# An encoder trunk in two blocks: the second block cut into three 368-column chunks that hold the sample tokens behind a zero gap

## The reference, cut to what matters

```python
def layer(x, pool_buf, conv_buf, ffn_buf, offset, ...):      # x: (B, T, 1024)
    h = rmsnorm(x, g_pre_mix)
    z = h @ w_in                                             # 2048 columns: v | gb | gc | u
    pooled, new_pool = multiscale_pool(z_v, pool_buf, offset) # trailing means of 2, 4, 8, 16 tokens
    ya = einsum(pooled, pool_mix) * pool_scale
    conv_out, new_conv = causal_dwconv(gc * u, conv_buf, conv_w)   # 3 taps
    yb = gb * conv_out
    mix = concat([head_rmsnorm(ya, 4, ...), head_rmsnorm(yb, 8, ...)]) @ w_out
    x = x + rmsnorm(mix, g_post_mix)
    h = rmsnorm(x, g_pre_ffn)
    up, new_ffn = causal_dwconv(h @ w_up, ffn_buf, ffn_conv_w)     # 3 taps over 5632 columns
    f = (silu(up[..., :2816]) * up[..., 2816:]) @ w_down
    x = x + rmsnorm(f, g_post_ffn)
    return x, new_pool, new_conv, new_ffn
```

## Time and profile before

| | |
|---|---|
| median of three runs | 3019.7 us |
| the profiled execution | 3020.9 us |
| its span on the slowest core (core 7) | 3019.3 us |
| PE busy | 2792.1 us (92%), 13920 matmuls |
| DVE busy | 1917.6 us (64%) |
| ACT busy | 1505.4 us (50%) |
| POOL busy | 1004.0 us (33%) |
| share of PE in the chain that ended last | 80% |

### The profile page before, as it was taken

How to read it: one execution, slowest core, us unless ns; L and a number is a source line. 1 busy time by engine, 2 the same in 40 slices (tenths; PEclk the granted TensorE clock), 3 DMA queues, 4 the chain that set the end, 5 groups by cost and what they waited for, 6 DMA issues and landing times.

```text
span 3019.3 us, 45417 instructions; the slowest of 8 cores (2990.8 to 3019.3 us)
## 1 busy us (share of the span) xinstructions
PE 2792.1 (92%) x13920; PEld 1259.8 (42%) x13920; DVE 1917.6 (64%) x2636; ACT 1505.4 (50%) x3141; POOL 1004.0 (33%) x1092
## 2 busy tenths in 40 slices
PE   3999999999999999996899998899988899988998
PEld 1444444444444444443344443344433444433443
DVE  3787368745776478745677545777357774467763
ACT  3754366435644375445644346544356443464443
POOL 3344054414343144404333224433043331343320
PEclk9999999999999999998988999988999999998889
DMA  8684267525673359456473334733154632437321
GB/s 165 102 143 77 46 108 127 92 49 102 101 121 67 67 95 156 77 122 122 71 115 60 50 65 77 123 66 61 33 102 82 104 64 44 84 66 126 59 41 61
DMA packets 203853, 263.75 MB, mean 87 GB/s; under 512 B 147040, under 2 KB 148832, under 8 KB 203616
## 3 DMA queue, kind: packets, MB, share of 16 engines
q0 software_dynamic: 52992, 189.82, 38.4%
q1 hardware_dynamic: 150624, 71.03, 11.3%
HBM read 406.70 MB, written 9.29 MB: 138 GB/s over the span
## 4 chain that ended last, share of the span: by engine, by line
PE 80%; DVE 6%; issue 5%; ACT 4%; DMA 2%; POOL 1%; SPq 0%; DVEq 0%; ACTq 0%; POOLq 0%
PE psum_all L366 80%; DVE sb_r L400 3%; ACT sb_r L384 3%; DMA sb_h<-sb_hs 2%; DVE sb_r L389 1%; ACT sb_tp L384 1%; POOL sb_r L389 1%; DVE sb_hs L400 0%; POOL sb_x L389 0%; DVE sb_tp L400 0%; ACT sb_ss L384 0%; SPq L516 0%; DMA sb_g<-gains 0%; DVEq L150 0%; DVE sb_x L389 0%
## 5 line engine op out<-in xcount | busy, mean ns | idle before, releaser
L366 PE MATMUL psum_all<-sb_h,sb_w 128*128 128x512 bf16 (+1 forms) x9600 | 1872.0, 358 | 141.4 <-DMA sb_h<-sb_hs 64.3
L366 PEld LDWEIGHTS psum_all<-sb_h,sb_w 128*128 128x128 bf16 x9600 | 838.5, 101 | 1147.6 <-issue 485.6
L400 DVE SCALAR_TENSOR_TENSOR sb_r<-psum_all,sb_vec,sb_r 128x1023 f32<-128x1023 f32 (+2 forms) x1216 | 1027.4, 851 | 327.4 <-ACT sb_cf L404 246.0
L389 POOL TENSOR_TENSOR sb_r<-sb_r 128x1088 bf16<-128x1088 f32 (+16 forms) x416 | 637.9, 1533 | 1223.1 <-ACT sb_r L384 808.1
L366 PE MATMUL psum_all<-sb_w,sb_r 128*128 128x512 bf16 (+1 forms) x4080 | 893.1, 381 | 13.3 <-ACT sb_r L384 11.1
L384 ACT ACTIVATE sb_r<-psum_all,sb_vec 128x1024 f32<-128x1024 f32 (+4 forms) x768 | 539.7, 738 | 346.8 <-PE psum_all L366 345.9
L366 PEld LDWEIGHTS psum_all<-sb_w,sb_r 128*128 128x128 bf16 (+1 forms) x4080 | 400.9, 99 | 496.6 <-issue 29.2
L384 ACT ACTIVATE sb_r<-sb_r 128x1024 f32<-128x1024 f32 (+6 forms) x376 | 314.3, 839 | 430.4 <-DVE sb_r L389 398.2
L414 POOL DMA_DIRECT2D sb_w<-wts x360 | 206.9, 575 | 497.9 <-PE psum_all L366 457.2
L400 DVE SCALAR_TENSOR_TENSOR sb_tp<-psum_all,sb_ss,sb_g 128x1024 f32<-128x1024 f32 x136 | 174.3, 1282 | 307.7 <-ACT sb_ss L384 271.5
L400 DVE SCALAR_TENSOR_TENSOR sb_r<-sb_r,sb_vec 128x512 bf16<-128x512 f32 (+3 forms) x320 | 250.1, 802 | 105.6 <-ACT sb_r L384 97.3
(11 more groups left out here) (44 smaller groups left out, 543.4 us busy)
## 6 DMA issues: line engine op xcount, KB each, us to landing
sb_w<-wts POOLq DMA_DIRECT2D x360, 512.0 KB, 6.6
sb_g<-gains SPq DMA_DIRECT2D x33, 512.0 KB, 5.3
sb_x<-xp SPq DMA_DIRECT2D x16, 512.0 KB, 5.4
yp<-sb_x SPq DMA_DIRECT2D x16, 512.0 KB, 2.7
sb_h<-sb_hs SPq DMA_TRANSPOSE x136, 3.1
sb_pm<-pm POOLq DMA_DIRECT2D x8, 128.0 KB, 3.0
sb_tp<-gains SPq DMA_DIRECT2D x1, 512.0 KB, 9.2
sb_vec<-vecs SPq DMA_DIRECT2D x1, 312.0 KB, 22.9
```

Of the source, the lines that this page charges most:

```text
L366: P.op(PE, lambda h: h.matmul(oa, la, ra, start=start, stop=stop), reads=[lv.r(llo, lhi), rv.r(rlo, rhi)], writes=[ov.r(olo, ohi)])
L389: P.op(eng, lambda h: h.tensor_tensor(oa, aa, ba, op), reads=[av.r(alo, ahi), bv.r(blo, bhi)], writes=[ov.r(olo, ohi)])
L400: P.op(DVE, lambda h: h.scalar_tensor_tensor(oa, aa, sc, ba, op0, op1), reads=reads, writes=[ov.r(olo, ohi)])
```

## The change

In the second block the sample now stands in the same column range as the prompt, behind a gap of 16 columns of zeros: 1024 + 16 + 64 = 1104 columns, cut into three chunks of 368. The separate sample parts and `u_sample` are gone. Mixer history of the sample is copied into the gap, so pooling and short convolution run over it as over any other column. For the up projection a chunk's product has 370 columns: two columns before the chunk are recomputed, so the taps read all they need from PSUM and the edge terms between chunks go (`lead_edges` is used in the first block alone). Two last columns of `sb_h` from the first block are kept in `sb_hh` for that purpose. The first two chunks of a pair of PSUM banks are read by one instruction, as 2 x 368 columns; the third chunk lies in bank 6 or 7 alone. The second block has four lead pairs, whose first part is two chunks and whose second part is the third chunk.

Also changed: the order of channel groups (1, 3, 2, 0 in place of 3, 2, 1, 0); the order of tiles in the second block (the sample's is seventh of nine, it was fifth); the last token tile's pre norm of each layer is deferred into the first step of the next z stage, and at the start of the program and between the blocks four tiles are deferred into its first steps; banks are taken by least recent use, and the first block's up projection and both down projections use all eight; the first weight loads wait for transposes, not for token loads.

```diff
-NLEAD = 5
+NLEAD = (5, 4)
+JORDER = (1, 3, 2, 0)
+GAP = 16
+KN = 368
...
+        gap3 = h3[:, :, HO + 1024:HO + 1024 + GAP]
+        P.op(DVE, lambda h: h.memset(gap3, 0.0), writes=[hv[kt].r(HO + 1024, HO + 1024 + GAP) for kt in range(KT)])
...
-                ts.insert(4, dict(x=8, a=1024, p=64, src=xs_d[:, :], dst=ys_d[:, :]))
+                ts.insert(6, dict(x=8, c=1024 + GAP, p=DSEQ, src=xs_d[:, :], dst=ys_d[:, :]))
...
+            bounds = (0, 512, 1024) if bi == 0 else (0, KN, 2 * KN, 3 * KN)
...
+                sched = ((0, 0), (1, 0), (0, 1), (1, 1), (0, 2), (2, 0), (1, 2), (2, 1), (3, 0), (2, 2), (3, 1), (3, 2))
...
+                    m.a_gc()
+                    if si < len(deferred):
+                        for f in deferred[si]:
+                            f()
...
-                def u_sample(i, ws, fg, fvv):
-                    for t_, fv in ((0, fg), (1, fvv)):
-                        jt = i + NPAIR * t_
-                        bk = banks[6 + t_]
-                        u_mm(i, ws, t_, bk, 0, 1024, 64)
-                        conv_ew(fv, 1024, 64, bk, 0, jt, (b_e, 88 + 2 * jt), (b_stf, (l * 44 + jt) * 2))
...
+                def conv_b(fv, k0, cnt, b0, jt):
+
+                    ps = V(b_ps, b0 * PBANK, cnt * PBANK, F32)
+                    out = spread(fv, k0 * KN, KN, cnt, KN)
+                    ract(out, shifted(ps, 2, cnt), AF.Copy, scale=vcol(l, W2 + jt))
...
+                    for w, sh in ((W1, 1), (W0, 0)):
+                        rstt(out, shifted(ps, sh, cnt), vcol(l, w + jt), out, ALU.mult, ALU.add)
+                    if k0 + cnt == 3:
+                        a = 1024 + GAP
+                        tt(DVE, (fv, a, a + 2), (fv, a, a + 2), (V(b_e, 2 * jt, 2, F32), 0, 2), ALU.add)
...
+                        if part != 1:
+                            pk = take_pair(range(3))
+                            for k in range(2):
+                                u_mm(ws, t_, banks[2 * pk + k], HO - 2 + k * KN, KN + 2)
+                            conv_b(fv, 0, 2, 2 * pk, jt)
+                        if part != 0:
+                            bk = take_bank((6, 7))
+                            u_mm(ws, t_, banks[bk], HO - 2 + 2 * KN, KN + 2)
+                            conv_b(fv, 2, 1, bk, jt)
...
-                    if not last_layer:
+                    if last_layer:
+                        final_tile(t, "pre", t["dst"])
+                    elif last:
+                        deferred = [[lambda t=t: pre_tile(t, "pre")]]
+                    else:
                         pre_tile(t, "pre")
```

More of the change, by code:

```diff
@@ L209, in unit_table @@
     tab = []
[L210 removed]
+    for j in JORDER:
         tab += [("z", 2 * j), ("z", 2 * j + 1)]
@@ L400, in stt, with __init__, spread, ract @@
             P.op(DVE, lambda h: h.scalar_tensor_tensor(oa, aa, sc, ba, op0, op1), reads=reads, writes=[ov.r(olo, ohi)])
+        class Raw:
+            def __init__(self, ap, rs):
+                self.ap, self.rs = ap, list(rs)
+        def spread(v, lo, n, cnt, stride):
+            o_ = v.off + lo
+            ap = v.b.t[0:v.p, o_:o_ + cnt * stride].rearrange("p (b c) -> p b c", c=stride)[:, :, 0:n] \
+                if o_ + cnt * stride <= v.b.width else None
+            assert ap is not None and v.dt == F32
+            return Raw(ap, [(v.b, o_ + k * stride, o_ + k * stride + n) for k in range(cnt)])
+        def ract(out, in_, func, scale=None, bias=None):
+            kw, reads = {}, list(in_.rs)
+            if scale is not None:
+                kw["scale"] = scale
+                if isinstance(scale, tuple):
+                    kw["scale"] = scale[0]; reads.append(scale[1])
+            if bias is not None:
+                kw["bias"] = bias[0]; reads.append(bias[1])
+            P.op(ACT, lambda h: h.activation(out=out.ap, in_=in_.ap, func=func, **kw), reads=reads, writes=out.rs)
+        def rstt(out, in0, scalar, in1, op0, op1):
+            P.op(DVE, lambda h: h.scalar_tensor_tensor(out.ap, in0.ap, scalar[0], in1.ap, op0, op1),
+                 reads=in0.rs + in1.rs + [scalar[1]], writes=out.rs)
         def copy(eng, out_ap, out_r, in_ap, in_r):
@@ new lines, in __init__ @@
+                        self.yp = yp[i % 2]
+                        self.sc = sqc[i % 2]
+                        self.sp = sqp[i % 2]
+                    def a_v(self):
+                        c, vb = self.c, self.vb
+                        va = 16 + c["c"]
+                        act((vb, va, va + self.n), (self.bv, 0, self.n), AF.Copy)
+                        with_s = c["last"] and bi == 1
+                        if with_s:
+                            state_in(POOL, b_stp, 15, self.j, vb, 16 + 1024 + GAP)
@@ L743, in d_fin, with do @@
                             ALU.mult, ALU.mult)
[L745 to L750 removed]
+                p1 = p2 = None
+                def do(p, *names):
+                    if p is not None:
                         for nm in names:
                             getattr(p, nm)()
[L754 to L755 removed]
+                for si, (pos, ci) in enumerate(sched):
+                    j = JORDER[pos]
+                    if ci == 0:
@@ new lines, in next_fa, with conv_a @@
+                def next_fa():
+                    fa_ctr[0] += 1
+                    return fa[fa_ctr[0] % 4]
+                def conv_a(fv, lo, n, src, jt, edge=None, tail=None):
+                    act((fv, lo, lo + n), (src, 0, n), AF.Copy, scale=vcol(l, W2 + jt))
+                    if tail is not None:
+                        copy(ACT, tail.ap(0, 2), tail.r(0, 2), src.ap(n - 2, n), src.r(n - 2, n))
+                    for w, sh in ((W1, 1), (W0, 2)):
+                        stt((fv, lo + sh, lo + n), (src, 0, n - sh), vcol(l, w + jt), (fv, lo + sh, lo + n),
+                            ALU.mult, ALU.add)
+                    if edge is not None:
+                        tt(DVE, (fv, lo, lo + 2), (fv, lo, lo + 2), (edge, 0, 2), ALU.add)
```

500 lines of the change are left out of this document (232 added, 268 removed).

## The result

The changed kernel takes 2908.6 us in the profiled execution and 2910.9 in a second one; its ratio to the kernel before is 0.9652, with a 95% interval of 0.9614 to 0.9691. In the other two of its four executions the cores of one die ran at a mean clock of 0.84 to 0.87, so the ratio leaves these two out, and all that follows is read from cores and stretches at full clock. Faster was forecast with 0.83, the time as 2880 us within 2845 to 2965.

The account below looks back on a forecast made before the run. The prediction took a loop through ACT and DVE to bound the second block's u. Its terms, -120 + 9 - 25 - 7 - 2 = -145, gave 2876 us on core 7; it forecast 2880 us for the slowest core, within 2845 to 2965.

Parts of the forecast that it names:

- The bound and the loop: Second block's u: PE waits for a loop through ACT and DVE, some 29 us a stage; the change leaves PE the bound.
- u, -120: Second block's four u stages: 684 us against 804.0, since the loop goes and PE is the bound.
- the third chunks: Lead pairs in second block's u: PE waits because only banks 6 and 7 serve; 0 to 5.6 us, 2.5 taken.
- DVE's backlog: Second block's u: 2 us a stage for DVE being behind from the norms.
- o and the start of u, +9: Second block, from o to u: 6.2 us wait for a tile's norm and transpose, 1.5 us low clock; bounds -18 to +25.
- z of layers 1 to 3, -25: Second block's z: 75 us each, 225 against 250.3, with a first pool-map wait of 4.3 us; bounds -50 to 0.
- z between the blocks, -7: Stage between the blocks: 90 us against 97.0, with waits of 16.4 us in place of 17.4; bounds -20 to +5.
- The rest, -2: Program start, first-block z and down projections: earlier chunk 0 offset by deferred tiles, last pre norm gives little; bounds -12 to +10.
- d, 0: Down projection stages: no change, since they are PE's, 343.4 of 345.6 us.
- The clock falls: Two rivals: low clock again in u, +34 us a stage, chance 0.22; or in all the second block, 3190 us, 0.04.
- DVE and ACT become the bound: Rival in u: each piece of a two-piece read costs its own 0.21 us; 2930 us if z keeps its time; chance 0.10.
- The loop stays: Rival in u: SiLU still waits, now on g's third chunk; u at 190 us, kernel 2956; chance 0.04.

Follow-up runs that it names:

- the first experiment: Kernel before, with only the sample piece of g moved ahead of v's work in the second block's u: 2926 to 2929 us, ratio 0.97.
- the eight banks: Changed kernel, with the second block's lead third chunks allowed any of eight PSUM banks instead of 6 and 7: 2881.5 and 2882.6 us, ratio 0.955.
- the products put ahead: Changed kernel, with first chunks of the first two lead pairs ahead of their second chunks at the second block's u start: 2904 and 2916 us, ratio 0.9689.
- the second profile: Changed kernel run once more without an edit, beside the kernel of three edits: 2903.3 to 2907.8 us.
- the narrow instructions: Changed kernel, with two-piece reads undone in the second block's u, each 368-column chunk having its own copy and taps: 2928 and 2932 us, ratio 0.9756.

## Why the prediction was right, and where its sizes were off

**The bound and the loop: right.** PE waited in u for a loop through ACT and DVE; order alone removes it, as the first experiment shows. What the prediction did not say is that its chunks would have hidden the loop even in the old order.

**u, -120: right in sum, in part by luck.** 171 us were forecast without the wait at the start. Measured are 179.2 with it; 5.8 of wait and some 2.5 behind it at a clock of 0.50 (16 to 20 matmuls of 308 instead of 156 ns) leave 171. Within that the third chunks were mis-sized: 2.5 us forecast, 5.7 by the eight banks, and the 2 us forecast for DVE's backlog did not come on top. The 2.5 rest on a misread row. For the wait of 5.26 us in the earlier trace rows the prediction blames POOL's edges, but DVE idled for them for 1.66 us of it:

```profile
1526.17 0.16 DVE L389 TENSOR_TENSOR sb_r<-sb_r,sb_lc 128x2 f32<-128x2 f32 x1 [1.66 <-POOL sb_lc L909]
```

For the rest DVE was at work on taps, until bank 6 was free for the next 64-column product. Two banks were too few in the kernel before as well.

**o and the start of u, +9: right.** 32.6 us for o (31.9 forecast), 5.8 us of wait (6.2 forecast), some 2.5 of low clock (1.5 forecast). The reason given, a norm and a transpose that lag, was half of it: with the products put ahead DVE was late instead.

**z of layers 1 to 3, -25: too much.** 78 us instead of 75. The first pool map waits 5.6, not 4.3; the later ones wait up to 0.94 us each behind DVE, some 3 us a layer, and 12 to 19 matmuls at the low clock cost 2 to 3 more, where 5 had been allowed for all of that.

**z between the blocks, -7: the step that failed.** 90 us were forecast, 102.6 measured on the slowest core. Of the deferred tiles the prediction priced the work on ACT and DVE and the wait for the sample's transpose, but it names no wait for the first deferred tile's transpose. On two cores that transpose landed about 14 us after its issue, and PE waited 7.7 and 7.84 us. The middle core had 92.3 us in this execution, but in the second profile five of the eight cores had 99.2 to 100.1. So it was not only the worst core that was mis-sized. Why the landing takes twice as long on some cores stays open.

**The rest, -2: 6 us longer.** On core 5 the first o starts at 119.0 us, where core 7 had 109.7 before; z of the first block gave 4 back. The prediction had the deferred tiles only take back what an earlier start gives.

**d, 0: 3 us better.** On core 7 of before d was mostly PE's already; on the cores without low clock 2.9 us a stage went with the loop.

Taken together, the sum of 2876 us was 32.6 too low: 12.6 between the blocks, 9 in the other z, 8 at the start and in the first block, 6 in o and u, less 3 in d. Three of its side sums do not come out either, without bearing on this: by its own terms core 5 gains 111 us and not 114, four o without a wait make -22 and not -18, and the chances add up to 1.00 without the 0.05 left below 2845.

**The rivals.** *The clock falls*: in none of the stages of the profiled execution. Of the Trainium skill's rule of 13/16 of the clock with three dense cores on a die ("TensorE: Matmul & The Clock Gate", Part 1) the profiled execution shows nothing, with all eight cores at 0.979 to 0.983. *DVE and ACT become the bound*: not here, but DVE at 149.9 of 179.3 us is near it, and the narrow instructions cross the line. *The loop stays*: it didn't, and where it was put back it cost nothing.

## What to carry to other kernels

When PE waits once in every round, find the loop of engines whose instructions are released by each other, and try its order before its shapes: one block of code moved gave three quarters of what a rewritten block gave. Judge a deferred step by its worst core and by more than one execution: a transfer that starts with little time to spare shows every spread of its landing, here 6.2 to 14.2 us over the cores of one execution. A wait that is moved on PE alone comes back at the next instruction of the same chain.

## What the runs showed of the hardware

A copy or tap that reads two pieces of 368 columns in neighbouring PSUM banks takes 875 and 984 ns, which lies on the line through the contiguous sizes of the earlier trace rows (0.87 and 0.98 us worked out for 736 columns); the same columns as two taps take 2 x 597 ns. One deferred transpose, the same instruction at the same place in the program, took 14.2 us from issue to landing on one core and 7.4 on another, and PE waited 7.84 and 0.17 us for it.
